# First layer of a four-layer transformer kernel: gate tiles finished half a pair later, and weight splits moved from ScalarE to GpSimd and VectorE

## The chip, the cores and the metric

One core of one Trainium2 chip runs the whole program. The number that counts is the device time of one execution in microseconds (us), here the median of three runs. A core has TensorE (PE; its weight loads are PEld), VectorE (DVE), ScalarE (ACT), GpSimd (POOL) and SyncE (SP, which here only issues the loads of weights).

## What is computed

Four transformer layers over 512 tokens of width 1024, all in float32. The first one, a sparse attention with three branches and a gate, is the one that the change touches. Cut to what matters:

```
q, kc, vc, ks, vs, kw, vw, gate, z = split(u @ w_in)      # u = rmsnorm(x)
o_c = attention over compressed keys                       # 31 blocks
o_s = attention over selected keys                         # here: causal, 16 heads
o_w = attention over a window of keys                      # here: causal, 16 heads
o   = gate0 * o_c + gate1 * o_s + gate2 * o_w
y   = (o * silu(z)) @ w_out
x   = x + rmsnorm(y)
```

`z` is a product of its own: 1024 columns of `u @ w_in`, passed through silu and multiplied into the attention's output.

Every float32 product is made of three fp32r products. A matrix `w` is split into `w_hi` (rounded) and `w_lo = w - w_hi`, and so is `u`, and `u_lo*w_hi + u_hi*w_lo + u_hi*w_hi` are added up in PSUM. So each weight tile that is loaded must be split by some engine before TensorE can use it: a high part (a copy that rounds) and a low part (a subtraction).

## The kernel before

**The flow of pairs.** The attention of the first layer (`nsa_flow`) runs in 64 steps: 8 pairs of heads, and for each pair 2 halves of the queries, 2 branches and 2 query tiles. Call the eight steps of a pair 0 to 7. Steps 0 to 3 (the *narrow half*) have 128, 256, 128, 256 keys, steps 4 to 7 (the *wide half*) have 384, 512, 384, 512. A step number i runs over all pairs, i = 8 * pair + step. For each step every engine does one piece, in program order of its own, and semaphores tie them:

- PE: `scores(i)`, three products for each of two heads (L1472)
- DVE: `score(i)`, adds the bias and takes the maximum (L1582); this sets `taken`
- ACT: `exps(i)` (L964)
- DVE: `inverse(i)` (L1588)
- POOL: `normalise(i)` (L1714)
- PE: `turn(i)`, transposes of the probabilities (L1500)
- ACT: `high(i)` (L1642), DVE: `low(i)` (L1594), the split of the turned probabilities
- PE: `values(d)`, the product with the values for steps 2d and 2d+1 (L1520, L1528)
- after every four steps ACT `low_out` (L1650), DVE `add_out` (L1602), and POOL `gate_out` (L1725, L1731, L1735), which multiplies by silu(z)

PE goes in rounds of two steps, i = 0, 2, 4, ...: `scores(i)`, `scores(i+1)`, `turn(i-3)`, `values(i/2-3)`, `turn(i-2)`, and then some chunks of z. ACT's step i is `exps(i-1)`, `high(i-3)`, perhaps `low_out`. DVE's step i is `low(i-4)`, perhaps `add_out`, `inverse(i-2)`, `score(i)`. POOL's step i is `normalise(i-2)` and perhaps `gate_out`, at the steps 1 and 2 of a pair. `values` at the start of a half waits until `add_out` has freed the PSUM bank (`out_sum`).

**The gate tiles.** z has 8 tiles of 128 columns, and each tile is 8 chunks of three matmuls of 512 columns (L1429, `z_fill`), 64 chunks in all, in PSUM bank 7 alone. So the first chunk of tile t waits (`z_taken`) until ACT has taken tile t-1 out of the bank with silu (`z_take`, L1458). Silu is in another table of ACT than the exponential: each `z_take` between `exps` costs two table loads, one before it and one before the next `exps`. 12 chunks stand ahead of round 0, 4 stand behind each of the rounds 0 and 2, and 2 behind every later one until they are used up, at i = 46. With that, tile t ends in round 8t-10, and `z_take(t)` stands at ACT's step 8t-7, which is step 1 of a pair.

**The weights of z** come in halves of 1024 columns of a slot, each asked for on SP's queue when the tile two before is done (`z_done`). ACT makes the high part in one instruction at step 2 of a pair (`z_high_part`, L1438), POOL the low part in two of 512 columns at steps 3 and 4 (`z_low_part`, L1447). The first two units of `nsa_out` (the output product) are loaded when all of z is done. ACT splits their high parts in 8 pieces of 512 columns at the steps 51 to 58 (L468), POOL their low parts in 16 pieces of 256 columns at the steps 53 to 68 (L479).

PE's `first_output` and the rest of `nsa_out` (L524) follow at the end of the flow.

## Time and profile before

| | us |
|---|---|
| median of 3 runs (lowest, highest) | 1406.35 (1405.98, 1406.77) |
| profiled execution, its own time | 1407.09 |
| its span on the core | 1405.3 |
| PE busy in the span | 1340.7 (95%) |
| ACT busy | 748.3 (53%) |
| DVE busy | 658.6 (47%) |
| POOL busy | 760.5 (54%) |
| mean granted TensorE clock | 0.994 |

The flow of pairs of the first layer lies between about 168 and 373 us of the span. A share of busy time over the whole span mixes stages with different limits, so the flow has to be read by itself: which engine waits there, for whom, and how long a pair takes. PE's busy time counts each matmul to its modelled end, so that neighbours overlap; starts of rows are surer than ends.

### The profile page before, as it was taken

How to read it: one execution, taken by the hardware profiler on the slowest of the kernel's cores; microseconds unless marked ns; L12 is line 12 of the kernel's file. 1: busy time of each engine (PE TensorE's matmuls, PEld its weight loads, DVE VectorE, ACT ScalarE, POOL GpSimd, SP SyncE). 2: the span in 40 equal slices, each digit the busy share in tenths (PEclk: the TensorE clock that was granted, in tenths of full speed). 3: DMA queues.
4: the chain of work that ended last, by engine and by line, in shares of the span. 5: the costliest groups of instructions: out<-in, count | busy, mean ns of one | idle time of the engine just before them, and what ended most of it. 6: DMA issues, size and time to landing. Idle time of an engine off the chain costs nothing.

```text
span 1405.3 us, 20958 instructions
## 1 busy us (share of the span) xinstructions
PE 1340.7 (95%) x7738; PEld 1095.5 (78%) x7738; DVE 658.6 (47%) x1617; ACT 748.3 (53%) x1576; POOL 760.5 (54%) x796
## 2 busy tenths in 40 slices
PE   6999989998999999999999999999999999999997
PEld 5878767776888787887788888778889887778885
DVE  4343456676351444554330011891463436887135
ACT  4253378878542465665442323893544355887252
POOL 4443256656744456665554425687555524586652
PEclk9999999999999999999999999999999999999999
DMA  6242001001424322221443223334316223002322
GB/s 234 90 151 90 30 31 61 31 29 64 149 91 150 132 79 76 90 76 61 150 180 120 90 98 111 130 112 165 105 62 229 108 89 72 2 16 102 139 90 60
DMA packets 28901, 138.66 MB, mean 99 GB/s; under 512 B 3584, under 2 KB 4096, under 8 KB 18048
## 3 DMA queue, kind: packets, MB, share of 16 engines
q1 hardware_dynamic: 15200, 98.05, 19.9%
q10 hardware_dynamic: 13600, 39.27, 8.0%
q8 instruction: 63, 1.03, 0.3%
q14 instruction: 38, 0.31, 0.1%
HBM read 127.86 MB, written 8.39 MB: 97 GB/s over the span
## 4 chain that ended last, share of the span: by engine, by line
PE 76%; DVE 7%; ACT 7%; POOL 4%; issue 2%; DMA 2%; SPq 0%; POOLq 0%; ACTq 0%; DVEq 0%
PE psum L524 47%; PE psum L558 9%; PE psum L1472 3%; PE psum L1429 3%; PE psum L1500 3%; PE psum L1520 3%; DVE w_free L1582 2%; PE psum L1078 2%; ACT w_free L964 2%; POOL w_lo L479 2%; PE psum L1052 2%; DMA w_raw<-in_weights 1%; PE psum L774 1%; PE psum L1485 1%; ACT x_r L1642 1%
## 5 line engine op out<-in xcount | busy, mean ns | idle before, releaser
L479 POOL TENSOR_TENSOR w_lo<-w_raw,w_hi 128x512 fp32r<-128x512 f32 (+2 forms) x163 | 389.8, 2405 | 279.8 <-ACT w_hi L468 270.1
L468 ACT ACTIVATE w_hi<-w_raw 128x2048 fp32r<-128x2048 f32 (+2 forms) x92 | 159.2, 1731 | 91.8 <-DMA w_raw<-in_weights 77.8
L524 PE MATMUL psum<-w_hi,split 128*128 128x512 f32 x608 | 195.1, 394 | 3.2 <-POOL w_lo L479 2.2
L524 PE MATMUL psum<-u_lo,w_hi 128*128 128x512 f32 (+1 forms) x428 | 169.2, 395 | 1.6 <-POOL w_lo L479 1.6
L524 PE MATMUL psum<-u_hi,w_lo 128*128 128x512 f32 (+1 forms) x428 | 166.8, 390 | 0.0
L524 PE MATMUL psum<-u_hi,w_hi 128*128 128x512 f32 (+1 forms) x428 | 166.8, 390 | 0.0
L964 ACT ACTIVATE w_free<-w_free,neg_max 128x512 f32<-128x512 f32 (+3 forms) x256 | 148.2, 584 | 10.0 <-DVE neg_max L1582 9.0
L524 PE MATMUL psum<-w_hi,u_lo 128*128 128x512 f32 (+2 forms) x352 | 134.2, 381 | 1.8 <-DVE u_lo L924 1.8
L524 PEld LDWEIGHTS psum<-w_hi,split 128*128 128x128 f32 x608 | 114.2, 188 | 27.5 <-POOL w_lo L479 3.0
L524 PE MATMUL psum<-w_hi,u_hi 128*128 128x512 f32 (+2 forms) x352 | 132.5, 377 | 0.0
L524 PE MATMUL psum<-w_lo,u_hi 128*128 128x512 f32 (+2 forms) x352 | 132.5, 376 | 0.0
L1500 PE MATMUL psum<-ident,w_free 128*128 128x128 f32 x704 | 109.6, 283 | 21.9 <-DVE w_lo L1594 7.7
L524 PE MATMUL psum<-w_lo,split 128*128 128x512 f32 x304 | 118.4, 390 | 0.0
L1500 PEld LDWEIGHTS psum<-ident,w_free 128*128 128x128 f32 x704 | 76.6, 141 | 49.3 <-issue 25.1
L1714 POOL TENSOR_SCALAR w_free<-w_free,inv,gate 128x256 f32<-128x256 f32 (+3 forms) x128 | 76.6, 608 | 67.5 <-DVE inv L1588 67.4
L1714 POOL TENSOR_SCALAR w_free<-w_free,inv 128x256 f32<-128x256 f32 (+1 forms) x128 | 73.2, 586 | 63.8 <-DVE inv L1588 63.8
L524 PEld LDWEIGHTS psum<-u_lo,w_hi 128*128 128x128 f32 (+1 forms) x428 | 79.8, 186 | 20.1 <-POOL w_lo L479 2.1
L524 PEld LDWEIGHTS psum<-u_hi,w_hi 128*128 128x128 f32 (+1 forms) x428 | 79.8, 187 | 17.6
L524 PEld LDWEIGHTS psum<-u_hi,w_lo 128*128 128x128 f32 (+1 forms) x428 | 79.9, 187 | 16.4
L1472 PE MATMUL psum<-split 64*128 64x512 f32 (+3 forms) x768 | 86.7, 349 | 5.0 <-DVE neg_max L1582 4.4
L1472 PEld LDWEIGHTS psum<-split 64*128 64x128 f32 x768 | 57.0, 185 | 30.8 <-issue 14.8
L524 PEld LDWEIGHTS psum<-w_hi,u_lo 128*128 128x128 f32 x352 | 66.4, 189 | 14.7 <-issue 3.6
(240 smaller groups left out, 2793.3 us busy)
## 6 DMA issues: line engine op xcount, KB each, us to landing
w_raw<-in_weights SPq DMA_DIRECT2D x83, 1024.0 KB, 4.8
x<-x_scratch ACTq DMA_DIRECT2D x12, 512.0 KB, 4.9
w_raw<-in_weights SPq DMA_DIRECT2D x10, 512.0 KB, 4.6
gain<-in_gains ACTq DMA_DIRECT2D x9, 512.0 KB, 5.2
gain<-in_strips ACTq DMA_DIRECT2D x16, 256.0 KB, 2.9
spare<-in_strips ACTq DMA_DIRECT2D x16, 256.0 KB, 2.8
x_scratch<-x ACTq DMA_DIRECT2D x8, 512.0 KB, 4.0
gain<-in_near ACTq DMA_DIRECT2D x8, 512.0 KB, 4.2
```

Of the source, the lines that this page charges most:

```text
L468: high = nc.scalar.activation(w_hi[b][:, c], w_raw[b][:, c], ACT.Copy)
L479: low = nc.gpsimd.tensor_tensor(w_lo[b][:, c], w_raw[b][:, c], w_hi[b][:, c].bitcast(F32), ALU.subtract)
L524: mm = nc.tensor.matmul(dst, lhs, rhs, start=(a == 0 and k == 0 and (wl, ul) == (0, 1)), stop=(a + 1 == u and k + 1 == nk and (wl, ul) == ...
L558: mm = nc.tensor.matmul(bank(tiles.bank(t)), w[b][:, c:c + P], u[:, k * T:(k + 1) * T], start=(k == 0 and nth == 0), stop=(k == KC - 1 and ...
L964: nc.scalar.activation(p_map(f, i, m, n), p_map(f, i, m, n), ACT.Exp, scale=-1.0, bias=stat_of(neg_max, i, m), accum_out=stat_of(row_sum, ...
L1052: mm = nc.tensor.matmul(bank(m, n), lhs, split[64 * m:64 * m + 64, b:b + n], start=(nth == 0), stop=(nth == 2))
L1078: mm = nc.tensor.matmul(head_bank(d, r), turned_place(i, n, low)[:, pt], split[:, a + v:a + v + P], start=(kt == 0 and nth == 0), stop=(kt ...
L1429: mm = nc.tensor.matmul(bank(Z_BANK), w[b][:, col:col + P], u[:, k * T:(k + 1) * T], start=(k == 0 and nth == 0), stop=(k == KC - 1 and nt ...
L1472: mm = nc.tensor.matmul(score_place(f, i, m), *products[m][nth], start=(nth == 0), stop=(nth == 2 and f is not mla_flow))
L1500: tr = nc.tensor.transpose(psum[:, 4 + m, kt * P:(kt + 1) * P], p_map(f, i, m, n)[:, kt * P:(kt + 1) * P], ident[:])
L1520: mm = nc.tensor.matmul(dst, value_place(f, d, m, kt), pt_pair(f, pt_step(f, 2 * d) // 2, low, m, a, b), start=(br == 0 and m == 0 and kt ...
L1714: nc.gpsimd.tensor_scalar(p_map(f, i, m, n), p_map(f, i, m, n), stat_of(inv, i, m), factor_of(f, i, m), ALU.mult, ALU.mult).then_inc(f.p, 1)
```

## The change

Three things are changed, all in the flow of pairs of the first layer.

1. **Rounds.** Behind every round from round 0 on stand 2 chunks of z (before: 4, 4, then 2). The chunks now reach to i = 50. Tile t ends in round 8t-6, and `z_take(t)` stands at ACT's step 8t-3: step 5 of a pair, in the wide half, and no longer step 1.
2. **Weights of z**, tiles 2 to 7. POOL makes the high part, in two instructions of 512 columns at the steps 7 and 0 of a pair (`z_high_half`), and DVE the low part, in two of 512 columns at the steps 1 and 2 (`z_low_half`). For tile 2 it is POOL's steps 2 and 3 and DVE's steps 4 and 5. ACT has none of it. Tiles 0 and 1 stay as they were.
3. **The two units of `nsa_out`.** POOL makes the high parts, 8 pieces of 512 columns at the steps 55 to 62, and DVE the low parts, 8 pieces of 512 columns at the steps 58 to 65. ACT has none of it.

```diff
-        Z_FIRST, Z_EARLY = KC + KC // 2, KC // 2
+        Z_FIRST = KC + KC // 2
+        OUT_STEP = 55
 
         def z_step(t):
 
-            return 1 if t == 1 else KC * t - 9
-
-        def z_round(d):
-
-            return (Z_FIRST + Z_EARLY * d, Z_EARLY) if d < 2 else (Z_FIRST + 2 * Z_EARLY + 2 * (d - 2), 2)
+            return KC * t - 5
+
+        def z_split_step(t):
+
+            return max(2, z_step(t - 2) + 4)
...
+        def z_high_half(pool, t, half):
+
+            b, c = SLOT[Z_UNIT], t % 2 * D + half * T
+            pool.wait_ge(z_loaded[t % 2], 16 * (t // 2 + 1))
+            high = nc.gpsimd.tensor_scalar(w_hi[b][:, c:c + T], w_raw[b][:, c:c + T], 1.0, 1.0, ALU.mult, ALU.mult)
+            if half == 1:
+                high.then_inc(z_high, 1)
+
+        def z_low_half(dve, t, half):
+
+            b, c = SLOT[Z_UNIT], t % 2 * D + half * T
+            dve.wait_ge(z_high, t + 1)
+            low = nc.vector.tensor_tensor(w_lo[b][:, c:c + T], w_raw[b][:, c:c + T], w_hi[b][:, c:c + T].bitcast(F32), ALU.subtract)
+            if half == 1:
+                low.then_inc(z_ready, 1)
...
-                    z_fill(pe, *z_round(i // 2))
+                    z_fill(pe, Z_FIRST + i, 2)
...
+                if f is nsa_flow:
+                    for t in range(2, KC):
+                        if i - z_split_step(t) - 2 in (0, 1):
+                            z_low_half(dve, t, i - z_split_step(t) - 2)
+                    if 0 <= i - OUT_STEP - 3 < 8:
+                        out_low_part(dve, NSA_OUT + (i - OUT_STEP - 3) // 4, (i - OUT_STEP - 3) % 4)
...
-                    for t in range(2, KC):
-                        if i == (z_step(t - 2) + 3 if t > 2 else 1):
-                            z_high_part(act, t)
-                    if 51 <= i < 59:
-                        split_high(act, NSA_OUT + (i - 51) // 4, (i - 51) % 4, 4)
...
-                if f is nsa_flow and i == 2:
-                    z_low_part(pool, 2, 0)
-                    z_low_part(pool, 2, 1)
...
-                    for t in range(3, KC):
-                        if i - z_step(t - 2) - 4 in (0, 1):
-                            z_low_part(pool, t, i - z_step(t - 2) - 4)
-                    if 53 <= i < 69:
-                        split_low(pool, NSA_OUT + (i - 53) // 8, (i - 53) % 8, 8)
+                    for t in range(2, KC):
+                        if i - z_split_step(t) in (0, 1):
+                            z_high_half(pool, t, i - z_split_step(t))
+                    if 0 <= i - OUT_STEP < 8:
+                        out_high_part(pool, NSA_OUT + (i - OUT_STEP) // 4, (i - OUT_STEP) % 4)
...
             pair_pool(pool, nsa_flow)
+            pool.wait_ge(w_ready, NSA_OUT + 2)
```

`out_high_part` and `out_low_part` are the same two instructions as `z_high_half` and `z_low_half`, on a quarter of a unit of `nsa_out`.

Three places of the program show what moved. First ACT, from the end of one pair into the next, in the kernel before. `L1458` is `z_take` with its table load, `L1438` the high part of a z tile, `L964` exps, `L1642` high, `L1650` low_out:

```order
119 L1642 ACTIVATE x_r<-psum 128x512 x2
120 L1458 ACT_TABLE_LOAD
121 L1458 ACTIVATE x<-psum 128x512
122 L964 ACT_TABLE_LOAD
123 L964 ACTIVATE w_free_68,row_sum<-w_free_68,neg_max 128x128 x2
124 L1642 ACTIVATE x_r<-psum 128x384 x2
125 L1650 ACTIVATE arena<-psum 64x512
126 L1438 ACTIVATE w_hi_55<-w_raw_63 128x1024
127 L964 ACTIVATE w_free_68,row_sum<-w_free_68,neg_max 128x256 x2
```

And in the changed kernel, where the take of the same tile (`L1487`) stands four steps later, ahead of the first exps of the wide half (`L1677` is high, `L1685` low_out):

```order
122 L1677 ACTIVATE x_r<-psum 128x128 x2
123 L964 ACTIVATE w_free_68,row_sum<-w_free_68,neg_max 128x256 x2
124 L1677 ACTIVATE x_r<-psum 128x256 x2
125 L1487 ACT_TABLE_LOAD
126 L1487 ACTIVATE x<-psum 128x512
127 L964 ACT_TABLE_LOAD
128 L964 ACTIVATE w_free_68,row_sum<-w_free_68,neg_max 128x384 x2
129 L1677 ACTIVATE x_r<-psum 128x128 x2
130 L1685 ACTIVATE arena<-psum 64x512
```

The take has moved from the head of the narrow half to the head of the wide half, and the high part of the weights has left the engine.

Second PE, round 2 of the first pair, in the kernel before: scores (`L1472`), turn(0) (`L1500`) and then four chunks of z (`L1429`), of which the first two stand here:

```order
635 L1472 MATMUL psum<-split 128x128 x6
636 L1472 MATMUL psum<-split 128x256 x6
637 L1500 MATMUL psum<-ident,w_free_68 128x128 x2
638 L1429 MATMUL psum<-u_lo,w_hi_55 128x512
639 L1429 MATMUL psum<-u_hi,w_lo_59 128x512
640 L1429 MATMUL psum<-u_hi,w_hi_55 128x512
641 L1429 MATMUL psum<-u_lo,w_hi_55 128x512
642 L1429 MATMUL psum<-u_hi,w_lo_59 128x512
643 L1429 MATMUL psum<-u_hi,w_hi_55 128x512
```

The same place in the changed kernel (`L1501` scores, `L1529` turn, `L1430` z), where the next round's scores follow behind two chunks:

```order
629 L1501 MATMUL psum<-split 128x128 x6
630 L1501 MATMUL psum<-split 128x256 x6
631 L1529 MATMUL psum<-ident,w_free_68 128x128 x2
632 L1430 MATMUL psum<-u_lo,w_hi_55 128x512
633 L1430 MATMUL psum<-u_hi,w_lo_59 128x512
634 L1430 MATMUL psum<-u_hi,w_hi_55 128x512
635 L1430 MATMUL psum<-u_lo,w_hi_55 128x512
636 L1430 MATMUL psum<-u_hi,w_lo_59 128x512
637 L1430 MATMUL psum<-u_hi,w_hi_55 128x512
638 L1501 MATMUL psum<-split 128x384 x6
639 L1501 MATMUL psum<-split 128x512 x6
```

The chunks that ended in this round of the kernel before are now spread over later ones; four chunks altogether have left the first pair.

Third POOL, where a wide half goes into the next narrow one, in the kernel before (`L1714` normalise, `L1725` to `L1735` gate_out, `L1447` a low part of z):

```order
50 L1714 TENSOR_SCALAR w_free_68<-w_free_68,inv,gate 128x512 x2
51 L1725 TENSOR_TENSOR arena<-arena,x 128x256
52 L1731 TENSOR_SCALAR split<-arena 128x256
53 L1735 TENSOR_TENSOR split<-arena,split 128x256
54 L1714 TENSOR_SCALAR w_free_68<-w_free_68,inv,gate 128x128 x2
55 L1725 TENSOR_TENSOR arena<-arena 128x256
56 L1731 TENSOR_SCALAR split<-arena 128x256
57 L1735 TENSOR_TENSOR split<-arena,split 128x256
58 L1714 TENSOR_SCALAR w_free_68<-w_free_68,inv,gate 128x256 x2
59 L1447 TENSOR_TENSOR w_lo_59<-w_raw_63,w_hi_55 128x512
```

And in the changed kernel (`L1744` normalise, `L1755` to `L1765` gate_out, `L1454` a high part of z):

```order
64 L1744 TENSOR_SCALAR w_free_68<-w_free_68,inv,gate 128x512 x2
65 L1454 TENSOR_SCALAR w_hi_55<-w_raw_63 128x512
66 L1744 TENSOR_SCALAR w_free_68<-w_free_68,inv,gate 128x384 x2
67 L1454 TENSOR_SCALAR w_hi_55<-w_raw_63 128x512
68 L1744 TENSOR_SCALAR w_free_68<-w_free_68,inv,gate 128x512 x2
69 L1755 TENSOR_TENSOR arena<-arena 128x256
70 L1761 TENSOR_SCALAR split<-arena 128x256
71 L1765 TENSOR_TENSOR split<-arena,split 128x256
72 L1744 TENSOR_SCALAR w_free_68<-w_free_68,inv,gate 128x128 x2
73 L1755 TENSOR_TENSOR arena<-arena 128x256
```

The two instructions on the z weights stand behind normalise of steps 5 and 6 instead of behind those of steps 1 and 2, and they are of another kind.

## Rows read from the trace of the kernel before

**Rows 1.** Busy time by stretch: range, length, PE, PEld, DVE, ACT, POOL, PEclk, DMA, GB/s

```profile
244.81:269.67 24.86, 22.82 (x170) 18.54 (x168) 16.23 (x61) 20.39 (x55) 15.76 (x25) 1.00 0.13 42
...
294.51:318.81 24.30, 22.55 (x170) 18.49 (x168) 16.31 (x61) 19.36 (x53) 13.22 (x23) 1.00 0.17 61
318.81:343.00 24.19, 19.27 (x144) 16.57 (x143) 15.89 (x59) 22.00 (x63) 15.78 (x27) 0.86 0.12 49
```

**Rows 2.** Timeline of PE, one pair: start, length, instruction, [idle before it, releaser]

```profile
245.55 0.47 PE L1429 MATMUL psum<-u_lo,w_hi 128*128 128x512 f32 x1 [0.56 <-ACT x L1458]
...
248.71 1.09 PE L1500 MATMUL psum<-ident,w_free 128*128 128x128 f32 x8 [0.65 <-DVE w_lo L1594]
250.08 0.36 PE L1520 MATMUL psum<-w_hi,split 128*128 128x256 f32 x1 [0.27 <-DVE arena L1602]
...
253.13 0.30 PE L1500 MATMUL psum<-ident,w_free 128*128 128x128 f32 x1 [0.30 <-DVE w_lo L1594]
...
256.19 0.66 PE L1500 MATMUL psum<-ident,w_free 128*128 128x128 f32 x4
...
262.08 0.36 PE L1520 MATMUL psum<-w_hi,split 128*128 128x256 f32 x1
...
266.57 1.09 PE L1500 MATMUL psum<-ident,w_free 128*128 128x128 f32 x8
267.42 0.36 PE L1520 MATMUL psum<-w_lo,split 128*128 128x256 f32 x1
```

**Rows 3.** Timeline of ACT, the same pair

```profile
243.52 1.28 ACT L1458 ACT_TABLE_LOAD   x1
...
245.43 1.28 ACT L964 ACT_TABLE_LOAD   x1
...
258.84 0.45 ACT L1642 ACTIVATE x_r<-psum 128x128 fp32r<-128x128 f32 x2 [0.33 <-PE psum L1500]
259.31 0.59 ACT L1650 ACTIVATE arena<-psum 64x512 f32<-64x512 f32 x1
```

**Rows 4.** Timeline of DVE, the same pair: `add_out` of the narrow half's first group

```profile
259.94 0.87 DVE L1602 TENSOR_TENSOR arena<-psum,arena 64x256 f32<-64x256 f32 x2 [0.29 <-ACT arena L1650]
```

**Rows 5.** Timeline of POOL, the same pair

```profile
244.50 1.52 POOL L1714 TENSOR_SCALAR w_free<-w_free,inv,gate 128x512 f32<-128x512 f32 x2 [2.25 <-DVE inv L1588]
...
250.23 0.88 POOL L1714 TENSOR_SCALAR w_free<-w_free,inv,gate 128x128 f32<-128x128 f32 x2 [2.19 <-DVE inv L1588]
...
254.21 1.28 POOL L1447 TENSOR_TENSOR w_lo<-w_raw,w_hi 128x512 fp32r<-128x512 f32 x1
```

**Rows 6.** Timeline of DVE, much later in the program: a subtraction with both inputs in SBUF

```profile
1027.99 4.72 DVE L2259 TENSOR_TENSOR arena<-arena 128x512 f32<-128x512 f32 x1 [2.51 <-ACT arena L2225]
```

**Rows 7.** Timeline of POOL at the same moment

```profile
1027.55 4.61 POOL L479 TENSOR_TENSOR w_lo<-w_raw,w_hi 128x2048 fp32r<-128x2048 f32 x1 [4.18 <-ACT w_hi L468]
```

**Rows 8.** POOL's line L1731: durations min/median/max in ns, first and last start, forms

```profile
L1731 POOL TENSOR_SCALAR split<-spare x24: 297/298/405, 898.0 to 961.7; 128x128 fp32r<-128x128 f32 x16, 128x256 fp32r<-128x256 f32 x8
```

**Rows 9.** Timeline of PE in the first pair and at the second's start

```profile
174.86 0.67 PE L1500 MATMUL psum<-ident,w_free 128*128 128x128 f32 x2 [1.25 <-POOL w_free L1714]
176.39 0.47 PE L1429 MATMUL psum<-u_lo,w_hi 128*128 128x512 f32 x1 [0.86 <-ACT arena L1458]
...
191.14 0.95 PE L1472 MATMUL psum<-split 64*128 64x128 f32 x12
```

**Rows 10.** Busy time by stretch, columns as in rows 1: round 2's four chunks

```profile
176.39:180.78 4.39, 4.39 (x13) 2.99 (x14) 0.56 (x3) 4.28 (x12) 0.88 (x2) 0.63 0.00 0
```

**Rows 11.** Timeline of PE in the seventh and eighth pair

```profile
314.84 0.95 PE L1472 MATMUL psum<-split 64*128 64x128 f32 x12
...
322.71 1.94 PE L1500 MATMUL psum<-ident,w_free 128*128 128x128 f32 x8 [2.83 <-DVE w_lo L1594]
...
337.65 0.55 PE L1472 MATMUL psum<-split 64*128 64x128 f32 x6
...
351.28 0.97 PE L1500 MATMUL psum<-ident,w_free 128*128 128x128 f32 x4 [1.27 <-POOL w_free L1714]
```

16 lines of the change are left out of this document (12 added, 4 removed).

## The prediction

> **What bounds the kernel now.** I read the busy time by stretch first, for the flow of pairs alone. A pair takes 24.86 us (from one z_take to the next) and PE is busy for 22.82 of it, the most of any engine; ACT has 20.39, DVE 16.23, POOL 15.76 [rows 1]. So PE sets the pace and what can be won is its idle time. Next the pair in PE's timeline, to see where that lies. All of it is in the narrow half: 0.56 us before the chunks of round 0, until z_take has emptied the bank; 0.65 before turn of step 7; turn itself, 1.37 us to the start of values (250.08 less 248.71) where the same eight transposes take 0.85 in the wide half (267.42 less 266.57); and 0.30 inside turn(0) [rows 2]. That is 0.56 + 0.65 + 0.52 + 0.30 = 2.0 us. From turn(1) at 256.19 to the start of values(0) at 262.08 PE is dense: 5.89 us [rows 2]. Third, ACT's timeline says why. z_take stands at the head of the narrow half and costs 245.43 + 1.28 - 243.52 = 3.19 us, two table loads with a silu between [rows 3], and then ACT makes the high part of the z weights. The wide half has room on ACT, it waits for PE there (0.33 us before the high of step 2) [rows 3].
>
> One row tests this at once. The sixth pair has no high part on ACT (19.36 us busy and not 20.39) and takes 24.30 us, 0.56 less [rows 1]. So a microsecond less on ACT in the narrow half is worth about 0.56 us of a pair.
>
> **The narrow half after the change.** z_take (3.19) and the high part (1.03, 20.39 less 19.36 [rows 1]) leave ACT here. PE's 2.0 us named above all end on ACT or on a DVE step behind it, and 4.2 us are taken out ahead of them, so I take all four as gone. What would be late next? The string on POOL. In the kernel before it runs from 244.50 to 254.21 with 2.19 us of idle inside [rows 5], so 7.5 us of work: normalise, gate_out, normalise, gate_out, normalise(1). DVE's part of a z weight has both inputs in SBUF. Such an instruction on DVE took 4.72 us from 1027.99 [rows 6] while POOL ran one of 4.61 us from 1027.55 [rows 7]: it ended 0.55 us after POOL's, so it had waited and then run. So DVE's two parts and POOL's instructions go one after the other: two times 0.55 = 1.1 us more in the string, 8.6 in all, and normalise(1) is done 8.6 us after 244.50, at 253.1. Turn(1), which needs it, comes at 256.19 less 2.0, at 254.2. It holds, with 1.1 us to spare; DVE itself was idle behind both places (POOL waits there for an inverse, not DVE for work).
>
> The Trainium skill (SBUF — State Buffer, Who interferes with whom) says of this that a VectorE instruction with two SBUF inputs takes the read interface which GpSimd uses, and that whoever comes second is blocked for the whole instruction. The row of 4.72 us agrees. By that rule the delay could be a whole instruction of POOL on DVE's side too, at most 0.7 us here, and it speaks against giving both engines work on the same weights.
>
> **The wide half after the change.** Here z_take comes in ahead of exps(4). Before, from turn(1) at 256.19 to low_out at 259.31 are 3.12 us [rows 2, 3], of which ACT waited 0.33 for PE [rows 3]: 2.79. With z_take: 2.79 + 3.19 = 5.98. From low_out's start to add_out's start 0.63 (259.94 less 259.31), add_out 0.87 [rows 3, 4], and some 0.15 until PE goes on (as at 250.08, where values waited for add_out [rows 2]). So values(0), which needs the bank that add_out frees, starts 5.98 + 1.65 = 7.63 us after turn(1), where PE would be there after 5.89 [rows 2]. PE waits 1.74 us that it did not wait before: at the z chunks of round 4, at turn(3) and at values(0). What follows (normalise(4), turn(4)) hangs on the same add_out and comes in time.
>
> So a pair wins 2.0 and loses 1.74: 0.26. The waits in rows are only those that the view gives; the scraps beside them (start of turn(0) to the chunks, gaps under 0.1) may be another 0.3. I take 0.4 a pair, 24.46, between 0 and 0.7. For the pairs two to six: PE's scores start at 191.14 [rows 9] for the second and at 314.84 [rows 11] for the seventh, 123.70 us. The sixth already had 0.56 of the gain. So 4 * 0.4, and the sixth, 24.30 against 24.46, 0.16 longer: -1.6 + 0.2 = **-1.4 us**. In words: leaving the high part to POOL is worth its 0.56, and moving z_take by itself costs 0.16.
>
> **The first pair.** Four of its chunks go elsewhere. At 176.39 to 180.78 four chunks took 4.39 us at a granted clock of 0.63 [rows 10], 1.10 a chunk. In the steady pair two take 1.56 (0.78 a chunk, from the chunks' start at 245.55 to the scores behind them at 247.11). Before them PE had stood 1.25 and 0.86 us [rows 9]. Without four chunks and without z_take and the high part ahead of exps, PE's work of the pair is 3.1 us shorter at full clock. But it is not all gain, for in the new order the two chunks of round 4 wait for DVE's second part (DVE's step 5, behind score(5)) and for z_take(1), which takes its 3.19 us there. Counted from the scores of round 0 (168.4) with the durations above, the chunks of round 4 start at about 180.6 and the second pair's scores at about 187.8, which is 3.4 us before 191.14. If the clock falls as it did before, and it may, since PE stands about 2.6 us of 3.1 before those chunks, 1.3 to 2.3 us of this are lost (4.39 less four times 0.78 is 1.3; the second fall of the kernel before, below, cost 2.3). I take the fall here, at 1.7: -3.4 + 1.7 = **-1.7 us**, ends -3.6 and -1.0.
>
> **The seventh pair.** It gets the four chunks, 3.1 us, and z_take at its step 5. It has 22.81 us now (314.84 to 337.65 [rows 11]), with a wait of 2.83 and turn of eight transposes at 1.94 in place of 1.09 behind it [rows 11]: the granted clock was 0.86 over 318.81 to 343.00 [rows 1], of two levels 1.2 and 2.4 GHz, so it stood at the lower for a good quarter of it. By the chain of the steady pair: turn(1) comes 13.1 us after the scores of round 0 (chunks included), values(0) 7.63 later, then 2.1 for values and turn(4) without chunks: 22.8. So **0**, ends -1.5 (ACT has five pieces less here) and +1.7 (PE would wait 2.3 and 0.9 us close together in its wide half, and the clock may fall).
>
> **The eighth pair and the end.** ACT loses its last pieces, and POOL's 16 low parts become 8 high ones. A high one of 512 columns: 298 ns for 128 and 405 for 256 columns [rows 8], 0.107 for each further 128, 0.62 us. A POOL low part of 512 was 1.28 [rows 5]. So POOL has 8 * 0.62 = 5.0 us where it had about 11.5 (16 at 0.72). Turn(1) there waited 1.27 us for POOL [rows 11]. But in the string ahead of it two low parts of 0.7 become two high ones of 0.62, and DVE's parts come in: about 0.3 us. **-0.3**, ends -2 and +1. The first two units of nsa_out are ready earlier than PE wants them in either kernel. The loads of z weights are asked for with each tile's end, four steps later, and POOL uses them five steps after that; 4 to 7 us of transfer against 12: hidden. The new wait on POOL ahead of the next chain is already met; behind it is the split of the next unit, which waits for ACT anyway.
>
> **Sum.** -1.7 - 1.4 + 0 - 0.3 = -3.4 us, against the profiled execution 1407.09 with its span of 1405.3. The median of the runs is 1406.35, 0.74 under it; the same difference applies to it: **1402.9 us**. A measurement of this kernel can tell about 0.2% from no change, 2.8 us, so the forecast stands just outside that.
>
> **Rivals.**
> 1. *The clock stays up* in the first pair, and the narrow half gives its scraps too: -3.4 - 2.6 - 0.5 - 0.5, 1399.4 us. For it: nothing in the steady pairs made it fall, with 2 us of waits in each narrow half. Chance 0.25.
> 2. *The wait only changes its place*: the narrow half's waits stay, taken over by POOL's string. From the 1.1 us to spare: if DVE's parts and POOL's instructions block each other by 0.55 to 0.6 us more for each, the pair is back at 24.86. The pairs two to six then give +0.6, the ends -2.0: 1405.0 us. By the skill's page above this is what a blocked instruction on either side would do. Chance 0.2.
> 3. *Both falls of the clock*, first and seventh pair: +1.7 on the forecast, 1404.6 us. Chance 0.15.
> 4. *Slower.* The three waits of the wide half, 1.74 us close together, pull PE's clock down in every pair, which the four scattered ones of the narrow half did not. Price: 1.3 to 2.3 us each time [rows 10, 11], on a path that is otherwise dense there; 1.5 * 5 = 7.5 on top of the forecast: 1410.4 us. It decides from the point where PE's waits between turn(1) and values(0) reach those that came before the two falls (1.25 and 0.86 close by, or 2.83 alone [rows 9, 11]); 1.74 is a little under. The Trainium skill (TensorE: Matmul & The Clock Gate, HAM oscillation — how this bites in real kernels) tells of a loop whose wait throws the clock back in each turn. No steady pair of this trace shows it (granted 1.00 [rows 1]). Chance 0.1.
>
> That the change doesn't do what it says is no case: the order of ACT, PE and POOL shows the moves.
>
> **How the numbers follow.** The forecast has 0.3. Range: from 1398.5 (case 1 with the narrow ends) to 1408.0 (case 2 with the bad ends); outside are case 4 and a part of case 1. Faster by over 0.2%, below 1403.5: about 0.6 of the forecast, all of case 1 and a part of 3: 0.52. Slower, above 1409.2: case 4 with the worst ends of 2, 0.1. Within: 0.38.
>
> **What will show it.** The distance from one z_take to the next: 24.3 to 24.6 in the pairs two to six. In the narrow half PE waits for DVE's low at turn of step 6 and for nothing else; in the wide half there are waits before the z chunks of round 4 (some 0.55), before turn(3) and before values(0) (about 1 us, ended by add_out). The second pair's scores stand at 187 to 190. ACT's busy time in a pair falls to 19.4, DVE's rises by 1.2. The granted clock tells cases 3 and 4. Wrong would be: a wait for POOL at turn(0) or turn(1) in the narrow half (case 2), low parts on DVE far over 0.7 us, or a pair over 24.9.

## The result

| | before | after |
|---|---|---|
| median (lowest, highest), 20 runs each | 1406.82 (1405.34, 1409.91) | 1409.98 (1407.71, 1412.38) |
| profiled execution, its own time | 1407.09 | 1407.71 |
| its span | 1405.3 | 1405.6 |
| mean granted TensorE clock in it | 0.994 | 0.995 |

The ratio is 1.0021, with a 95% interval of 1.0014 to 1.0028: the changed kernel is slower by 3 us, just beyond what a measurement of this kernel tells from no change. 1402.9 us was predicted, 1398.5 to 1408.0 as its range, and 0.1 was given to slower. Both the time and the sign were missed, and not through the rival that ended on the slow side.

The profiled execution of after is the shortest of its 20 runs, 2.3 us under their median. The medians have to be explained by the profile and by what differs between runs, and these are taken apart below.

### The profile page after: what moved, and what is told of

The parts are those of the page before. It is cut to its first block, busy times and chain, and to the rows that moved or that the text cites. A ratio compares the mean times of both kernels' runs of the same rounds, so it can differ in the third digit from the quotient of the medians.

```text
span 1405.6 us, 20957 instructions
## 1 busy us (share of the span) xinstructions
PE 1340.8 (95%) x7738; PEld 1096.0 (78%) x7738; DVE 670.9 (48%) x1637; ACT 738.8 (53%) x1562; POOL 752.4 (54%) x788
## 4 chain that ended last, share of the span: by engine, by line
PE 78%; DVE 8%; ACT 6%; POOL 4%; issue 2%; DMA 1%; SPq 0%; POOLq 0%; ACTq 0%; DVEq 0%
PE psum L524 48%; PE psum L558 9%; PE psum L1501 3%; PE psum L1529 3%; PE psum L1430 3%; PE psum L1549 3%; DVE w_free L1611 2%; PE psum L1078 2%; PE psum L1052 2%; POOL w_lo L479 1%; PE psum L774 1%; POOL w_free L1744 1%; PE psum L1514 1%; ACT w_free L964 1%; DVE arena L918 1%
## 5 line engine op out<-in xcount | busy, mean ns | idle before, releaser
L479 POOL TENSOR_TENSOR w_lo<-w_raw,w_hi 128x512 fp32r<-128x512 f32 (+2 forms) x147 | 378.1, 2587 | 276.9 <-ACT w_hi L468 267.6
L468 ACT ACTIVATE w_hi<-w_raw 128x2048 fp32r<-128x2048 f32 (+2 forms) x84 | 154.2, 1835 | 89.9 <-DMA w_raw<-in_weights 76.0
L964 ACT ACTIVATE w_free<-w_free,neg_max 128x512 f32<-128x512 f32 (+3 forms) x256 | 148.4, 585 | 11.9 <-DVE neg_max L1611 10.7
L1744 POOL TENSOR_SCALAR w_free<-w_free,inv,gate 128x256 f32<-128x256 f32 (+3 forms) x128 | 82.5, 654 | 99.6 <-DVE inv L1617 99.1
L1529 PE MATMUL psum<-ident,w_free 128*128 128x128 f32 x704 | 109.0, 283 | 19.8 <-DVE w_lo L1623 6.3
L1529 PEld LDWEIGHTS psum<-ident,w_free 128*128 128x128 f32 x704 | 76.6, 142 | 46.6 <-issue 25.3
L1744 POOL TENSOR_SCALAR w_free<-w_free,inv 128x256 f32<-128x256 f32 (+1 forms) x128 | 73.2, 586 | 63.8 <-DVE inv L1617 63.8
L1501 PE MATMUL psum<-split 64*128 64x512 f32 (+3 forms) x768 | 88.4, 355 | 5.0 <-DVE neg_max L1611 4.4
L1501 PEld LDWEIGHTS psum<-split 64*128 64x128 f32 x768 | 58.2, 188 | 31.2 <-issue 15.1
```

The costliest lines, as they stand in the source:

```text
L468: high = nc.scalar.activation(w_hi[b][:, c], w_raw[b][:, c], ACT.Copy)
L479: low = nc.gpsimd.tensor_tensor(w_lo[b][:, c], w_raw[b][:, c], w_hi[b][:, c].bitcast(F32), ALU.subtract)
L964: nc.scalar.activation(p_map(f, i, m, n), p_map(f, i, m, n), ACT.Exp, scale=-1.0, bias=stat_of(neg_max, i, m), accum_out=stat_of(row_sum, ...
L1501: mm = nc.tensor.matmul(score_place(f, i, m), *products[m][nth], start=(nth == 0), stop=(nth == 2 and f is not mla_flow))
L1529: tr = nc.tensor.transpose(psum[:, 4 + m, kt * P:(kt + 1) * P], p_map(f, i, m, n)[:, kt * P:(kt + 1) * P], ident[:])
L1744: nc.gpsimd.tensor_scalar(p_map(f, i, m, n), p_map(f, i, m, n), stat_of(inv, i, m), factor_of(f, i, m), ALU.mult, ALU.mult).then_inc(f.p, 1)
```

## The profile after

Lines have moved: `z_fill` is L1430, `scores` L1501, `turn` L1529, `values` L1549, `z_take` L1487, `low` L1623, `add_out` L1631, `high` L1677, `normalise` L1744. The new parts are `z_high_half` L1454, `z_low_half` L1462, `out_high_part` L1470 and `out_low_part` L1478.

Busy time by stretch of after, the columns as in [rows 1]. The stretches go from a pair's scores of round 0 to the next pair's: first, second, fourth, seventh. Then the eighth pair and the end, in three pieces, up to PE's long run of `nsa_out` products at 374.28:

```profile
168.88:189.75 20.87, 17.06 (x109) 12.54 (x108) 12.69 (x52) 15.11 (x45) 8.48 (x15) 0.92 0.09 26
189.75:213.86 24.11, 22.58 (x170) 18.50 (x169) 17.01 (x62) 19.18 (x53) 13.13 (x21) 1.00 0.14 45
237.98:262.09 24.11, 22.57 (x169) 18.50 (x168) 17.40 (x63) 19.35 (x55) 15.25 (x25) 1.00 0.15 45
310.31:333.02 22.71, 19.56 (x157) 16.42 (x156) 14.68 (x58) 17.95 (x52) 12.11 (x21) 1.00 0.31 117
333.02:345.00 11.98, 8.82 (x76) 7.41 (x75) 8.72 (x30) 8.49 (x26) 10.97 (x18) 1.00 0.00 1
345.00:360.00 15.00, 10.88 (x72) 8.76 (x72) 13.28 (x45) 10.17 (x31) 9.82 (x15) 0.87 0.00 1
360.00:374.28 14.28, 14.28 (x90) 13.17 (x89) 5.78 (x11) 3.75 (x7) 7.27 (x10) 0.89 0.20 71
```

The same stretch in the kernel before:

```profile
337.65:373.02 35.37, 30.89 (x236) 26.44 (x235) 22.27 (x76) 23.89 (x69) 30.50 (x48) 1.00 0.08 29
```

The steady pair did better than predicted: 24.11 us against 24.86 in [rows 1], ACT 19.35 against 20.39, DVE up by 1.17. The eighth pair with the end takes 11.98 + 15.00 + 14.28 = 41.26 us, against 35.37. That is +5.9 us, and the granted clock, 1.00 before, is 0.87 and 0.89 in its two later pieces. In this profiled execution the loss of the change is in this one place.

The longest groups of PE's waits in the eighth pair and the end, before and after the change (each line: what waited, for what, us in total, times, longest). Before:

```profile
PE psum L1500 <- DVE w_hi L1594: 2.5, 3, 1.2
PE psum L1500 <- POOL w_free L1714: 1.3, 1, 1.3
```

After, with DVE's own wait among them:

```profile
PE psum L1529 <- DVE w_lo L1623: 4.2, 3, 2.3
DVE w_lo L1478 <- POOL w_hi L1470: 3.5, 2, 2.5
PE psum L1529 <- DVE w_hi L1623: 2.5, 2, 2.2
```

PE's waits for POOL are gone, 1.3 us, and 4.2 us for DVE's low part (`low`, ahead of a `turn`) are new: +2.9 us. (The 2.5 us for DVE's `w_hi` stay, but nearly all of them are now one wait of 2.2 us, where the longest was 1.2.) DVE is late because it has itself stood for POOL. The timelines of POOL and then of DVE at the first of these places, step 58:

```profile
338.73 0.62 POOL L1470 TENSOR_SCALAR w_hi<-w_raw 128x512 fp32r<-128x512 f32 x1
339.31 0.73 POOL L1755 TENSOR_TENSOR arena<-arena 128x256 f32<-128x256 f32 x1
...
341.35 0.88 POOL L1744 TENSOR_SCALAR w_free<-w_free,inv,gate 128x128 f32<-128x128 f32 x2
342.20 0.62 POOL L1470 TENSOR_SCALAR w_hi<-w_raw 128x512 fp32r<-128x512 f32 x1
```

```profile
342.85 1.20 DVE L1478 TENSOR_TENSOR w_lo<-w_raw,w_hi 128x512 fp32r<-128x512 f32 x1 [2.46 <-POOL w_hi L1470]
343.98 1.27 DVE L1623 TENSOR_TENSOR w_lo<-psum,x_r 128x512 fp32r<-128x512 f32 x2
```

And PE's timeline behind them:

```profile
344.80 0.30 PE L1529 MATMUL psum<-ident,w_free 128*128 128x128 f32 x1 [2.27 <-DVE w_lo L1623]
345.40 0.30 PE L1529 MATMUL psum<-ident,w_free 128*128 128x128 f32 x1 [0.30 <-DVE w_lo L1623]
356.58 0.85 PE L1529 MATMUL psum<-ident,w_free 128*128 128x128 f32 x6 [1.61 <-DVE w_lo L1623]
```

The first low piece of a unit (DVE, step 55 + 3 = 58) waits for `w_high`, and POOL raises `w_high` (the semaphore for high parts) only with the unit's last high piece, which stands at POOL's step 55 + 3 = 58 too. Ahead of that piece POOL has the `gate_out` of step 57 (339.31 on) and the `normalise` of step 58. So DVE stands 2.46 us and then makes a piece that took 1.20 us, while its `low`, for which the next `turn` waits, is queued behind both. At step 62, the second unit, the same happens again (1.08 us of DVE, 1.61 of PE). The falls of the clock cost at most 0.13 * 15.00 + 0.11 * 14.28 = 3.5 us more. Together this accounts for the 5.9: 2.9 of waits and about 3 of clock. That the clock's part hangs on this one wait is not shown; e4 below speaks against it.

## The experiments

The experiments ran in three sets, e1 to e4, e5 to e8 and e9 to e11, each beside the kernel before on one chip (33, 35 and 15 runs of before); ratios are to these. "First pair" and so on are distances in the profiled execution between the scores of round 0 in PE's timeline; "the end" reaches to the long run of `nsa_out` products.

| kernel | median | ratio, 95% interval | profiled | first pair | third pair | seventh | eighth, end |
|---|---|---|---|---|---|---|---|
| before | | | 1407.09 | 22.77 | 24.86 | 22.81 | 35.37 |
| after | 1409.98 | 1.0021 (1.0014, 1.0028) | 1407.71 | 20.87 | 24.12 | 22.71 | 41.26 |
| e1 out split back | 1409.61 | 1.0022 (1.0012, 1.0033) | 1408.07 | 19.37 | 24.10 | 29.84 | 35.59 |
| e2 only out split | 1412.16 | 1.0035 (1.0022, 1.0047) | 1412.16 | 21.24 | 24.84 | 21.72 | 41.48 |
| e3 low parts later | 1407.48 | 0.9999 (0.9990, 1.0008) | 1405.29 | 20.84 | 24.11 | 23.73 | 36.27 |
| e4 wait by piece | 1407.92 | 1.0005 (0.9995, 1.0014) | 1410.23 | 20.82 | 24.11 | 24.53 | 39.76 |
| e5 out split back, late | 1406.54 | 0.9998 (0.9987, 1.0010) | 1410.44 | 23.37 | 24.11 | 24.54 | 38.29 |
| e6 high parts on ACT | 1405.24 | 0.9986 (0.9977, 0.9994) | 1407.38 | 23.38 | 24.12 | 24.54 | 36.51 |
| e7 old engines | 1407.08 | 1.0003 (0.9994, 1.0011) | 1409.82 | 21.60 | 24.24 | 24.23 | 40.28 |
| e8 only z engines | 1404.27 | 0.9984 (0.9975, 0.9992) | 1405.85 | 22.81 | 24.30 | 22.12 | 35.38 |
| e9 after again | | | 1411.35 | 20.85 | 24.11 | 24.54 | 42.55 |
| e10 first pair | 1404.42 | 0.9977 (0.9968, 0.9986) | 1406.97 | 19.80 | 24.14 | 23.61 | 36.56 |
| e11 last take | 1399.33 | 0.9943 (0.9931, 0.9955) | 1399.15 | 18.17 | 24.13 | 19.84 | 37.08 |

### Where the loss is: e1 and e2

**e1** is the changed kernel with the old split of the two first units of `nsa_out`:

```diff
 (vector)
-                    if 0 <= i - OUT_STEP - 3 < 8:
-                        out_low_part(dve, NSA_OUT + (i - OUT_STEP - 3) // 4, (i - OUT_STEP - 3) % 4)
 (scalar)
+                    if 51 <= i < 59:
+                        split_high(act, NSA_OUT + (i - 51) // 4, (i - 51) % 4, 4)
 (gpsimd)
-                    if 0 <= i - OUT_STEP < 8:
-                        out_high_part(pool, NSA_OUT + (i - OUT_STEP) // 4, (i - OUT_STEP) % 4)
+                    if 53 <= i < 69:
+                        split_low(pool, NSA_OUT + (i - 53) // 8, (i - 53) % 8, 8)
```

> The changed kernel with only the two first units of nsa_out split as before (high parts on ACT at steps 51 to 58, low parts on POOL at steps 53 to 68). Theory A (the loss of the changed kernel lies in the eighth pair, and comes from DVE standing in its own order for the high parts that POOL makes): the way from the eighth pair's scores to PE's first long run of nsa_out products falls from 41.4 us back to 35 to 36, the second to seventh pairs stay at 24.1 us each, and the time is 1402 to 1404.5 us. Rival B (the loss in the median comes from the new places of the gate tiles, whose waits pull the clock down in pairs that the profiled run does not show): the eighth pair may mend, but the median stays at 1407 us or more.

Measured: the eighth pair and the end fell to 35.59 us, as theory A wants, but the seventh pair rose to 29.84 and the median did not move (1409.61). ACT's timeline names the cause:

```profile
325.92 0.63 ACT L468 ACTIVATE w_hi<-w_raw 128x512 fp32r<-128x512 f32 x1 [8.12 <-DMA w_raw<-in_weights]
```

ACT stood 8.12 us for the load of the unit. Its slot is the one that the last z tiles are in, and in the new rounds these end later; the old step 51 is too early for the load. This part of the change can't be undone by itself, and the median of e1 says nothing on rival B. What e1 does show is that the eighth pair's loss goes with the split of `nsa_out`. It also shows the first pair of the changed kernel without a fall of the clock (granted 1.00 from 173 to 192 us): 19.37 us.

**e2** is the kernel before with the new split of `nsa_out` alone (the wait on `w_ready` ahead of the next chain too):

```diff
 (scalar)
-                    if 51 <= i < 59:
-                        split_high(act, NSA_OUT + (i - 51) // 4, (i - 51) % 4, 4)
 (gpsimd)
-                    if 53 <= i < 69:
-                        split_low(pool, NSA_OUT + (i - 53) // 8, (i - 53) % 8, 8)
+                    if 0 <= i - OUT_STEP < 8:
+                        out_high_part(pool, NSA_OUT + (i - OUT_STEP) // 4, (i - OUT_STEP) % 4)
 (vector)
+                    if 0 <= i - OUT_STEP - 3 < 8:
+                        out_low_part(dve, NSA_OUT + (i - OUT_STEP - 3) // 4, (i - OUT_STEP - 3) % 4)
```

> The kernel before with only the two first units of nsa_out split as in the change (high parts on POOL from step 55, low parts on DVE from step 58). Theory A: the eighth pair is 4 to 6 us longer than before and everything ahead of it is as before: 1410 to 1413 us. Rival B: within 1.5 us of before, 1405.5 to 1408 us.

Measured: 1412.16 us; the eighth pair and the end take 41.48 us, 6.1 more than before, and the second pair to the sixth are as before. The first and the seventh are 1.5 and 1.1 shorter than in the profile of before, though their code is the same: in the first the clock did not fall here (granted 1.00 from 168 to 190 us). The waits in the eighth pair are those of after, to a tenth:

```profile
PE psum L1513 <- DVE w_lo L1607: 4.2, 3, 2.3
DVE w_lo L1462 <- POOL w_hi L1454: 3.5, 2, 2.5
```

Theory A holds for the eighth pair, from both sides. Rival B is not refuted by this; e9 to e11 return to it. (Line numbers differ: L1462 is `out_low_part` here.)

### Wait or work: e3 and e4

**e3** is the changed kernel with DVE's low parts two steps later, **e4** the changed kernel with a wait for each piece by itself:

```diff
 (e3)
-                    if 0 <= i - OUT_STEP - 3 < 8:
-                        out_low_part(dve, NSA_OUT + (i - OUT_STEP - 3) // 4, (i - OUT_STEP - 3) % 4)
+                    if 0 <= i - OUT_STEP - 5 < 8:
+                        out_low_part(dve, NSA_OUT + (i - OUT_STEP - 5) // 4, (i - OUT_STEP - 5) % 4)
 (e4)
-            if part == 3:
-                pool_high.then_inc(w_high, NSA_OUT - Z_UNIT + 1 if n == NSA_OUT else 1)
+            pool_high.then_inc(z_high, 1)
...
-            dve.wait_ge(w_high, n + 1)
+            dve.wait_ge(z_high, KC + 4 * (n - NSA_OUT) + part + 1)
```

> The changed kernel with DVE's eight low parts of nsa_out two steps later (five steps behind POOL's high parts and not three), so that POOL has two steps more to end a unit. Theory A in its narrow form (it is the wait): DVE waits for POOL at most 0.3 us, the eighth pair and the end fall from 41.4 to about 36.5 us, time 1403 to 1405.5 us. Theory A in its wide form (it is the eight parts themselves, 0.7 to 1.2 us of DVE each, ahead of the low parts that PE's turns need): 39 us or more are left, time 1407 or more.

> The changed kernel with DVE's low parts of nsa_out in their places, each waiting only for the high part of its own quarter and not for the unit's last. Narrow form of theory A (it is the wait): 36.5 us for the eighth pair and the end, 1403 to 1405.5 us, as when the parts come two steps later. Wide form (it is the work of the parts): 39 us or more, 1407 or more. If this one is quick and the later parts are not, or the other way round, the place of the parts counts too.

Measured, e3: the profiled execution took 1405.29 us and the eighth pair and the end 36.27, as the narrow form says; DVE does not stand for POOL there. The waits of PE in e3 from 333 to 375 us, in the view of waits:

```profile
PE psum L1529 <- DVE w_hi L1623: 2.5, 2, 2.3
PE psum L1529 <- POOL w_free L1744: 2.1, 2, 1.7
```

The 4.2 us for DVE's low part are gone altogether, and the stretch has a clock of 0.99:

```profile
333.99:370.26 36.27, 31.06 (x235) 26.86 (x235) 27.06 (x80) 21.95 (x62) 27.10 (x41) 0.99 0.08 28
```

In e4 they are gone too (PE waits 2.7 us for POOL and 2.5 for DVE's `w_hi`), but the stretch took 39.76 us, which is what the wide form gave. The granted clock in it was 0.90, so that at most 0.10 * 39.76 = 4.0 us of it are the clock's. So at least as much clock is lost here, without the wait for the whole unit, as in after (0.92 over its 41.26 us).

By their medians (1407.48, 1407.92) both kernels lie 2 to 2.5 us above what the narrow form gave and at the lower end of the wide form's "1407 or more". The narrow form was worked out from the profiled execution of after, and the distance of that from its median was in none of the expectations. What is measured: against before, the ratio falls from 1.0021 to 0.9999 and 1.0005 when DVE no longer waits for POOL, 2 to 3 us, with all eight pieces still on DVE. So the wait cost 2 to 3 us of the median. What the pieces themselves cost is not shown by a run of its own: e5 below takes them off DVE but gives POOL 16 parts for them, and its median is 0.9 us under e3's, with intervals that overlap.

Over all profiles, the eighth pair kept its clock where the longest wait of PE in it was 1.3 us (before, e1 and e8: granted 1.00). In the ten others its longest wait is between 2.2 and 2.5 us, for DVE or for POOL, and behind such waits the clock fell in nine; e3 is the one where it did not.

### What differs between runs of the same kernel: e9

**e9** is the changed kernel once more, unchanged.

> The changed kernel once more, for a second profile of it. The 20 runs of it have a median 2.3 us above its profiled one, and runs with a lower mean clock take longer. In e5 and e6, whose first pair is the same program, that pair took 23.37 and 23.38 us and not 20.87, with a granted clock of 0.72 in 180 to 192 us. If the first pair is where the runs part, this profile shows it at about 20.9 or about 23.4 us, and the rest as in the first profile within 1 us but for the seventh and eighth pair, whose clock may also fall (each 1 to 3 us). If the spread comes from somewhere else, the first pair stays at 20.9 while the span changes.

Measured: one execution, 1411.35 us, 3.6 above the first profile. The first pair took 20.85, no difference, so the expectation's own guess fell. The seventh took 24.54 in place of 22.71, the eighth and the end 42.55 in place of 41.26, and the rest of the program 1.0 more. Stretches of e9, seventh pair, and the eighth with the end in two pieces:

```profile
309.82:334.36 24.54, 21.84 (x159) 18.45 (x158) 15.38 (x60) 18.54 (x52) 13.86 (x23) 0.88 0.28 108
334.36:360.00 25.64, 20.98 (x145) 17.26 (x144) 19.51 (x64) 16.65 (x50) 18.39 (x29) 0.83 0.00 1
360.00:376.90 16.90, 15.07 (x92) 13.89 (x91) 8.05 (x17) 5.65 (x12) 8.01 (x11) 0.82 0.18 61
```

In the first profile the clock was 1.00 through the seventh pair; here it was 0.88, behind the same wait of 2.15 us for DVE's low part. The first profile of after, then e9:

```profile
329.38 0.63 PE L1529 MATMUL psum<-ident,w_free 128*128 128x128 f32 x4 [2.15 <-DVE w_lo L1623]
```

```profile
328.88 1.09 PE L1529 MATMUL psum<-ident,w_free 128*128 128x128 f32 x4 [2.15 <-DVE w_lo L1623]
```

One and the same wait is followed by a fall in one run and by none in another. Over the 20 runs of after the mean clock goes from 0.990 to 0.995, and the times with it: the ten runs at 0.990 and 0.991 took 1409.3 us or more, the seven at 0.994 and 0.995 took 1407.7 to 1409.7. Of the 83 runs of before in the three sets 48 had 0.995 or more, of the 20 of after five. Seven profiles here have this wait and the same steps around it (after, e3, e4, e5, e6, e9, e10): the pair took 22.71 us once and 23.61 to 24.54 in the six others. (e7 has the wait too, with other weight splits ahead of it, and took 24.23.) The first profile of after was the one that was spared.

The Trainium skill (TensorE: Matmul & The Clock Gate, HAM oscillation — how this bites in real kernels) tells of a kernel whose PE waits for data in every pass and starts each next one at the low clock. These traces agree that the clock falls behind waits, and add that waits of 2.2 us, shorter than those of 3 to 5 us that the page shows, are followed by a fall in most profiles but not in all, and that those of 0.46 and 0.73 us in the steady pairs are followed by none (granted 1.00).

### Do the engines of the nsa_out split matter: e5 and e6

**e5** is e1 with ACT's parts at steps 55 to 62 and POOL's at 56 to 71. **e6** is e3 with the eight high parts on ACT:

```diff
 (e5, scalar; gpsimd likewise from 53 to 56)
-                    if 51 <= i < 59:
-                        split_high(act, NSA_OUT + (i - 51) // 4, (i - 51) % 4, 4)
+                    if 55 <= i < 63:
+                        split_high(act, NSA_OUT + (i - 55) // 4, (i - 55) % 4, 4)
 (e6, scalar)
+                    if 0 <= i - OUT_STEP < 8:
+                        out_high_part(act, NSA_OUT + (i - OUT_STEP) // 4, (i - OUT_STEP) % 4)
 (e6, gpsimd)
-                    if 0 <= i - OUT_STEP < 8:
-                        out_high_part(pool, NSA_OUT + (i - OUT_STEP) // 4, (i - OUT_STEP) % 4)
```

> The changed kernel with the two first units of nsa_out split by ACT (high) and POOL (low) as in the kernel before, but ACT's parts at steps 55 to 62 and POOL's at 56 to 71, since at step 51 ACT stood 8.12 us for their load. It asks whether the engines of this split matter once the load has landed and nobody stands for a whole unit. From the seventh pair's scores to PE's long run of nsa_out products the kernel before took 58.2 us, the changed one 64.0, the one with DVE's parts two steps later 60.0. Theory A (it was the order of the waits, not the engines): 59 to 61 us here, 1405 to 1408 us in time. Rival (POOL's 16 low parts of 0.7 us are too much for its string, which the change relieved): turns wait for POOL by 3 us or more, 62 us or more, 1409 or above.

> The changed kernel with DVE's low parts of nsa_out five steps behind (as e3) and the eight high parts at the same steps 55 to 62 on ACT, not POOL. In the eighth pair of e3 PE's turns wait 1.70 and 0.44 us for POOL's normalise while ACT has some 7 us of idle. Theory: these 2.1 us go, 58 us from the seventh pair's scores to the long run of nsa_out products, 1403.5 to 1406 us. Rival: ACT's parts of 0.63 us each stand ahead of its exps and its high parts for the turns, and the same time comes back as waits for DVE behind ACT: 60 us, 1406.5 to 1408.5.

Measured, e5: 1406.54 us, inside theory A's range, and 1.0 us under e3's median with intervals that overlap. Its profiled execution was one of the three slowest of twelve (1410.44), with 24.54 + 38.29 = 62.8 us for both pairs, and there PE did wait 3.5 us for POOL, as the rival said. So POOL's 16 parts are felt, but cost no more in the median than the other split. That this part of the change relieves POOL is true, and it brings nothing measurable. Both pairs together missed their 59 to 61 us and fell to the rival's side (62 or more), with the clock down in both.

e6: 1405.24, ratio 0.9986, under before with its whole interval. PE's waits for POOL fell from 2.1 us to 0.4, as expected. The 58 us expected for both pairs were missed: 24.54 + 36.51 = 61.05, in an execution whose clock fell in both. View of waits, 336 to 373 us:

```profile
PE psum L1529 <- DVE w_hi L1623: 2.6, 2, 2.2
PE psum L1549 <- DVE arena L1631: 0.5, 2, 0.3
PE psum L1529 <- POOL w_free L1746: 0.4, 1, 0.4
```

Against e3 (0.9999) it is 1.8 us better, with intervals that just overlap: ACT, rather than POOL, seems to be the engine with time in the eighth pair.

### What the steady pair's gain is made of: e7 and e8

**e7** is e3 with the z weights split by ACT and POOL at the new places, which takes both z_take and ACT's high part (now at step 7 of a pair) out of the narrow half, **e8** the kernel before with the z weights of tiles 3 to 7 split by POOL and DVE (tile 2 stays as it was, since PE wants it in round 2, before DVE's step 4):

```diff
 (e7, scalar: at the split step; gpsimd: the low halves at the next two)
+                        if i == z_split_step(t):
+                            z_high_part(act, t)
 (e8, gpsimd)
+                        if i - z_step(t - 2) - 3 in (0, 1):
+                            z_high_half(pool, t, i - z_step(t - 2) - 3)
 (e8, vector)
+                        if i - z_step(t - 2) - 5 in (0, 1):
+                            z_low_half(dve, t, i - z_step(t - 2) - 5)
```

> e3 (the changed kernel with DVE's nsa_out parts five steps behind) with the z weights split by ACT and POOL as before, at the new places: high on ACT at the split step, low on POOL at the next two. It leaves the new rounds and the later end of a tile alone. If the engines of the split are worth what the sixth pair of the kernel before told (1.03 us of ACT for 0.56 us), a pair takes 24.5 to 24.7 us where e3 has 24.11, and the time is 2 to 3 us above e3's, 1409 to 1411. If the later end of the tiles alone makes the gain, since it takes z_take and the split out of the narrow half: 24.1 to 24.2 us a pair and e3's time, 1406.5 to 1408.5.

> The kernel before with the z weights of tiles 3 to 7 split by POOL (high) and DVE (low) at nearly their steps; rounds, ends of tiles and the nsa_out split stay. By the prediction's step (0.56 us for the high part taken off ACT in the narrow half) a pair takes 24.3 us in place of 24.86 in the second to fifth pair, and the time is 2 us under before, 1404 to 1405.5. Rival (DVE and POOL block each other on the weights in the narrow half, where POOL's string has little room): 24.7 to 24.9 us, within 1 us of before.

Measured: 24.22 us a pair in e7 and 24.30 in e8. One pair of each:

```profile
262.93:287.15 24.22, 22.59 (x171) 18.50 (x170) 16.05 (x60) 20.19 (x56) 15.70 (x24) 1.00 0.13 44
```

```profile
215.27:239.57 24.30, 22.55 (x169) 18.49 (x168) 17.23 (x63) 19.35 (x54) 14.43 (x24) 1.00 0.14 45
```

| a pair | us | to before |
|---|---|---|
| before | 24.86 | |
| engines alone (e8) | 24.30 | -0.56 |
| rounds, ends of tiles and the later place of the split, old engines (e7) | 24.22 | -0.64 |
| both (after) | 24.11 | -0.75 |

Each is worth most of it alone, and the two together add little, because both empty the same place, the narrow half. In e7 it is emptied although ACT's work in a pair is hardly less (20.19 us, before 20.39). e7's whole time is inside its second case, 1406.5 to 1408.5 (1407.08); its seventh and eighth pair stand at a clock of 0.93 and 0.87 in the profile. Its first case, 24.5 to 24.7 a pair, fell, e8's 24.3 held, and e8 as a whole gave 1404.27 (ratio 0.9984), 2.7 us better against before than e7: its z_take stays at step 1 of the pair, and its seventh pair (22.12 us) and eighth (35.38) are like those of before.

### The waits at both ends of the flow: e10 and e11

**e10** is e6 with two steps of the first pair moved, **e11** is e10 with the last `z_take` moved:

```diff
 (e10, vector)
                     inverse(i - 2)
+                if f is nsa_flow and i == 4:
+                    z_low_half(dve, 2, 0)
+                    z_low_half(dve, 2, 1)
 (e10, scalar)
                     exps(act, f, i - 1)
+                    if f is nsa_flow and i == 4:
+                        z_take(act, 1)
 (e11, scalar)
-                        if i == z_step(t) + 2:
+                        if i == (z_step(t) + 2 if t < KC - 1 else 65):
                             z_take(act, t)
```

> e6 with the first pair's waits taken away: z_take(1) one step earlier and behind exps, in a stretch of 3.4 us in which ACT is idle, and the low part of tile 2 on DVE at step 4 ahead of score, where DVE is idle for 3 us. In e6 PE stood 1.49 us at the first chunks of tile 2 and the granted clock fell behind it. If these waits are what pulls the clock down: the first pair takes 18 to 19.5 us (20.8 to 23.4 in the six runs with the old order), the runs' mean clock rises from 0.993 to 0.995 or more and the median falls by 2 to 3.5 us, to 1402 to 1403.5. If the clock falls for another reason (the waits of 1.25 and 0.98 us that stay), the pair is only shorter by the wait itself, 1.5 us, and the time 1403.5 to 1405.

> e10 with the last tile's z_take (two table loads and a silu, 3.19 us of ACT) moved from the seventh pair, where PE waits 2.15 and 0.73 us around it, to step 65, where ACT stands 4.1 us. If z_take is what PE waits for there: the seventh pair falls from 22.7 (24.5 where the clock fell) to 19.5 to 20.5 us, the eighth and the end stay within 0.7 us, and the time is 2.5 to 4 us under e10's. If the wait of DVE's low part has another cause (PE is short of work in a pair without chunks), the seventh pair stays above 21.5 us and the time within 1 us of e10's.

Measured, e10: 1404.42 us, inside the second reading (the pair is shorter by its wait only). Its ratio is 0.0009 better than e6's, 1.3 us, with intervals that overlap, and the mean clock of its runs did not rise (six of ten at 0.992 or 0.993). The waits of the first pair are a part of the spread at most: with the old order it took 20.8 to 20.9 us in four profiles, 23.4 in two and 19.37 in one (e1), which the expectation had left out.

e11: 1399.33 us, all five runs between 1399.15 and 1400.14, ratio 0.9943. The runs of every other kernel here span 4.2 us or more. The seventh pair of e10, with z_take in it, and of e11 (windows laid to within 0.05 us of the pair):

```profile
312.68:336.29 23.61, 20.46 (x157) 17.23 (x156) 15.39 (x59) 18.88 (x53) 13.04 (x22) 0.96 0.31 112
```

```profile
308.30:328.10 19.80, 19.50 (x159) 16.39 (x158) 14.65 (x58) 14.79 (x48) 12.19 (x21) 1.00 0.37 134
```

ACT's load falls by 4.1 us, PE's waits (2.15 and 0.73 us around z_take in e10) are gone, and the clock is 1.00. In its new place z_take stands in ACT's idle time, and of its two table loads one is left, since no exps follows:

```profile
353.28 1.28 ACT L1487 ACT_TABLE_LOAD   x1
354.58 0.60 ACT L1487 ACTIVATE gain<-psum 128x512 f32<-128x512 f32 x1
357.21 0.88 ACT L1680 ACTIVATE x_r<-psum 128x384 fp32r<-128x384 f32 x2 [2.03 <-PE psum L1529]
```

The eighth pair pays 0.5 for it (37.08 against 36.56). Expected were 2.5 to 4 us under e10; the medians are 5.1 apart. The surplus fits the clock: in six of the seven profiles with the seventh pair's wait the clock fell with it, and here there is no wait. So rival B was true as well, for the seventh pair: the new place of the last gate tile costs the median what the first profile of after did not show. e11, whose five runs are few, beats both kernels.

## Why the prediction was wrong, step by step

| term | predicted | measured | in the profiled executions |
|---|---|---|---|
| start of the flow | 0 | +0.5 | 168.88, before 168.37 |
| first pair | -1.7 | -1.9 | 20.87, before 22.77 |
| pairs two to six | -1.4 | -3.1 | 120.56, before 123.70 |
| seventh pair | 0 | -0.1 | 22.71, before 22.81 |
| eighth pair and the end | -0.3 | +5.9 | 41.26, before 35.37 |
| rest of the program | 0 | -1.0 | 1031.32, before 1032.28 |
| span | -3.4 | +0.3 | |
| median less span | +1.05 | +4.4 | 1409.98 less 1405.6 |

The changes in the start and in the rest of the program can't be told from what differs between profiles: over the thirteen profiles the rest goes from 1031.2 to 1034.0 us, and the flow starts at 168.2 to 172.3, with the same code there but for one wait ahead of the next chain.

**The step that failed is "The eighth pair and the end".** It added up POOL's string, and POOL's waits did go. It then said that the units are ready earlier than PE wants them, and that looked at their end only. It did not ask what DVE's eight new instructions wait for, and what stands behind them on DVE. The diff shows both: `dve.wait_ge(w_high, n + 1)` in `out_low_part`, `w_high` raised for `part == 3` only, the first low piece at OUT_STEP + 3 and the fourth high piece at OUT_STEP + 3. The wait is for a piece on another engine that has a gate_out of some 2 us and a normalise right ahead of it. The prediction gave the new wait on `w_ready` ahead of the next chain a sentence and this one, inside the flow and ahead of `low`, none. e2 shows the price of the new split alone (+6.1 us in the stretch), e3 takes the wait away (-5.0 in the stretch, 36.27 for 41.26; 2 to 3 us of the median). With the wait gone the kernel is level with before (e3, 0.9999) and still 4.6 us over the forecast; most of that is the second step.

**Second, the step from span to median.** "The same difference applies to it" made the median 0.74 us lower than the profiled execution; for after it is 2.3 higher. Three us of the miss of 7.1 are this; half a microsecond of the three lies in the base, since the 20 runs of before have their median at 1406.82 and the three that the prediction used had 1406.35. e9 shows where most of them come from: the wait of 2.15 us in the seventh pair and those in the eighth are followed by a fall of the clock in most profiles, and the first profile was one with fewer. The prediction had a wait of 2.3 us close to one of 0.9 there, with a fall as the bad end of its range (+1.7, measured in e9 as +1.8). It took the middle, 0, where the profiles say that the fall is the rule.

**Third, the pairs two to six were mis-sized, on the good side.** Of the wide half the prediction was right to the hundredth: turn(1) at 226.64 and values(0) at 234.29 are 7.65 us apart, 7.63 was worked out from [rows 2 to 4]. Of its three waits two are where it put them, ahead of the z chunks and of values(0); turn(3), at 232.93, waits for next to nothing:

```profile
229.83 0.47 PE L1430 MATMUL psum<-u_lo,w_hi 128*128 128x512 f32 x1 [0.46 <-ACT gain L1487]
...
232.93 0.63 PE L1529 MATMUL psum<-ident,w_free 128*128 128x128 f32 x4
...
234.29 0.36 PE L1549 MATMUL psum<-w_hi,split 128*128 128x256 f32 x1 [0.73 <-DVE arena L1631]
```

The narrow half gave more than the 2.0 us of its waits. The starts of PE's scores, before and then after, show it:

```profile
240.84 0.95 PE L1472 MATMUL psum<-split 64*128 64x128 f32 x12
247.11 0.95 PE L1472 MATMUL psum<-split 64*128 64x128 f32 x12
254.76 1.50 PE L1472 MATMUL psum<-split 64*128 64x384 f32 x12
```

```profile
213.86 0.95 PE L1501 MATMUL psum<-split 64*128 64x128 f32 x12
219.34 0.95 PE L1501 MATMUL psum<-split 64*128 64x128 f32 x12
225.22 1.49 PE L1501 MATMUL psum<-split 64*128 64x384 f32 x12
```

The two rounds took 6.27 and 7.65 us and take 5.48 and 5.88: 2.56 us less. The idle times in the rows were 0.56 and 1.47, and each is some 0.2 to 0.3 short, because a row's idle time counts from the modelled end of the matmul before, which lies behind the real gap's start. (The distances are measured; that the modelled end is the reason is only inferred.) Of these 0.56 us more the prediction had taken 0.14 (0.4 for 0.26), and the wide half's two rounds cost 1.83 and not 1.74: 0.56 - 0.14 - 0.09 = 0.33 a pair, five times, is the 1.7 by which the term was missed. And "leaving the high part to POOL is worth its 0.56, and moving z_take by itself costs 0.16" was right in its first half (e8) and wrong in its second: with the old engines on the split, z_take and the split's later place gain 0.64 (e7), and added to the new engines they still gain 0.19 (24.30 to 24.11). The two were taken as a sum where they share one place. No run moves z_take by itself.

**The first pair** came as worked out: -1.9 against -1.7, with waits of 1.25, 0.99 and 1.49 us and a clock of 0.92. Its two parts hold as well: without a fall the pair was to be 3.4 us shorter than the 22.77 of before, and in e1, where the clock did not fall, it took 19.37, which is 3.4 less; the fall was taken at 1.7 and costs 1.5 (20.87 against 19.37). Which of the two a run gets was luck, for before too (22.77 with a fall, 21.24 in e2 without one). **The seventh** was 22.8 and measured 22.71, with the 2.3 and 0.9 us of waits at 2.15 and 0.73.

**The lock between DVE and POOL** (rival 2) is there, at the size that was taken, and does not decide. DVE's low parts took 0.82 and 0.85 us (the shortest of this line 0.69), and POOL's normalise beside them 1.95 and 1.31 where [rows 5] has 1.52 and 0.88:

```profile
217.53 1.95 POOL L1744 TENSOR_SCALAR w_free<-w_free,inv,gate 128x512 f32<-128x512 f32 x2 [1.39 <-DVE inv L1617]
221.47 1.31 POOL L1744 TENSOR_SCALAR w_free<-w_free,inv,gate 128x128 f32<-128x128 f32 x2
```

That is 0.86 us of the string, 1.1 was taken; turn(0) and turn(1) of the narrow half wait for nobody. The Trainium skill (SBUF — State Buffer, Who interferes with whom) says that a VectorE instruction with two SBUF inputs and a GpSimd instruction that reads SBUF keep each other out; these rows agree, and show the delay of both sides.

**Rival 4** (slower, through the wide half's waits in every pair) did not happen: the granted clock is 1.00 in every steady pair of every kernel here, with waits of 0.46 and 0.73 us in those of the changed one. The change was slower in good part through falls of the clock all the same, in the last two pairs, where one wait alone is over 2 us.

## What to carry to other kernels

When a step with a wait moves to another engine, write down which instruction of the other engine releases it, at which step that stands, and what is queued behind the waiter; two parts "three steps apart" stand in the same step when the first raises its semaphore only with its fourth piece. Gains of two edits that empty the same stretch of the critical engine do not add up, and one alone may give most of it. Before rearranging the steady loop, look at the short passes at its ends: a switch of ACT's tables moved from a pair without cover to idle time behind the last exps went with 5 us, more than the 3.1 us of everything that was done to the five steady pairs.

## What the runs showed of the hardware

A wait of PE of 2.15 us was followed by a fall of its clock in six of seven profiled executions with the same steps and not in the seventh (after: granted 1.00 and 22.71 us, or 0.88 and 24.54). In the eighth pair waits of 2.2 to 2.5 us were followed by one in nine profiles of ten, and waits of 1.3 us or less in none of three. The kernels with such waits have a spread of 4 to 7 us between their runs, and a single profile can lie at either end. Without the one in the seventh pair (e11) five runs lie within 1 us, though one of 2.18 us is left in the eighth. No fall stands behind the waits of 0.46 and 0.73 us in any steady pair.

The profiled execution need not stand near the median: 2.3 us below it in after, 3.9 above it in e5. For changes of a few tenths of a per cent the distances inside stretches at an undisturbed clock (24.11, 24.22, 24.30 us a pair; the first was 24.10 to 24.14 in nine profiles) tell more than the whole time does.
